# Stick-breaking heads: the triangle products from two float32r parts, in whole banks, at the end of their step

## What is computed

```python
z = jnp.einsum('bhtd,bhsd->bhts', qf, kf) * scale
mask = s_pos < t_pos
log_keep = jnp.where(mask, jax.nn.log_sigmoid(-z), 0.0)
later = lax.cumsum(log_keep, axis=3, reverse=True) - log_keep
w = jnp.where(mask, jnp.exp(jax.nn.log_sigmoid(z) + later), 0.0)
out = jnp.einsum('bhts,bhsd->bhtd', w, vf)
```

## Time and profile before

| | us |
|---|---|
| median of 3 runs | 3109.47 |
| lowest and highest | 3108.03, 3111.07 |
| the profiled execution | 3111.8 |
| its span, first to last instruction | 3110.0 |
| TensorE busy in the span | 3060.9 |
| VectorE, ScalarE, GpSimd busy | 1855.5, 1148.2, 1903.9 |
| mean granted TensorE clock | 0.997 |

### The profile page before, as it was taken

The page is one execution under the profiler, slowest core; times in us unless marked ns, Lnnn a source line. Parts: engine busy times, 40 slices in busy tenths (PEclk is TensorE's granted clock), DMA queues, the critical chain, the costliest instruction groups (busy, mean ns, idle before and its releaser), DMA issues.

```text
span 3110.0 us, 42623 instructions
## 1 busy us (share of the span) xinstructions
PE 3060.9 (98%) x15287; PEld 2585.1 (83%) x15287; DVE 1855.5 (60%) x3298; ACT 1148.2 (37%) x2064; POOL 1903.9 (61%) x1796
## 2 busy tenths in 40 slices
PE   8999999999999999999999999999999999999999
PEld 6877788887668888878777888999999997888887
DVE  7674544316765442250672236679857878987886
ACT  3455322102552221120554212434357763333333
POOL 7432666677337666766433566578875565667663
PEclk9999999999999999999999999999999999999999
DMA  7210222222212222222112222488888889999995
GB/s 229 73 41 28 102 95 95 95 95 102 75 42 102 95 95 95 95 102 95 68 55 75 69 95 106 166 284 300 299 303 310 331 317 371 374 375 362 360 361 205
DMA packets 153709, 539.26 MB, mean 173 GB/s; under 512 B 11155, under 2 KB 64564, under 8 KB 117172
## 3 DMA queue, kind: packets, MB, share of 16 engines
q1 hardware_dynamic: 97296, 334.78, 30.3%
q0 software_dynamic: 36864, 134.23, 11.8%
q10 hardware_dynamic: 19364, 67.72, 5.8%
HBM read 479.16 MB, written 57.40 MB: 173 GB/s over the span
## 4 chain that ended last, share of the span: by engine, by line
PE 93%; DVE 3%; DMA 1%; issue 1%; ACT 1%; SPq 1%; POOL 0%; ACTq 0%; DVEq 0%; POOLq 0%
PE banks L194 82%; PE banks L2831 3%; PE banks L2174 1%; PE banks L2212 1%; DMA weights_raw<-in_weights 1%; PE banks L1110 1%; PE banks L1197 1%; PE banks L1169 1%; PE banks L2191 1%; PE banks L1179 1%; PE banks L2775 1%; DVE memory L1887 0%; SPq L2712 0%; DVE memory L1882 0%; DVE memory L1873 0%
## 5 line engine op out<-in xcount | busy, mean ns | idle before, releaser
L194 PE MATMUL banks<-memory,weights_split 128*128 128x512 f32 (+1 forms) x9456 | 2070.7, 376 | 18.5 <-DVE memory L555 11.7
L194 PEld LDWEIGHTS banks<-memory,weights_split 128*128 128x128 f32 x9456 | 1714.8, 188 | 296.8 <-issue 37.5
L3405 POOL TENSOR_SCALAR weights_split<-weights_raw 128x512 fp32r<-128x512 f32 x576 | 374.8, 660 | 790.2 <-PE banks L194 397.1
L3410 POOL TENSOR_TENSOR weights_split<-weights_raw,weights_split 128x512 fp32r<-128x512 f32 x576 | 769.2, 1346 | 0.0
L3271 POOL TENSOR_TENSOR weights_split<-weights_raw,weights_split 128x512 fp32r<-128x512 f32 x384 | 506.2, 1341 | 302.9 <-ACT weights_split L3115 301.6
L194 PE MATMUL banks<-weights_split,memory 128*128 128x512 f32 (+1 forms) x2880 | 647.4, 386 | 0.6 <-POOL weights_split L3271 0.6
L194 PEld LDWEIGHTS banks<-weights_split,memory 128*128 128x128 f32 x2880 | 534.0, 188 | 110.3 <-POOL weights_split L3271 1.4
L3115 ACT ACTIVATE weights_split<-weights_raw 128x1024 fp32r<-128x1024 f32 x256 | 269.4, 1053 | 103.4 <-DMA weights_raw<-in_weights 66.9
L690 DVE TENSOR_TENSOR banks<-banks,memory 128x512 f32<-128x512 f32 x88 | 61.3, 699 | 231.9 <-PE banks L194 231.8
L2903 DVE CUSTOM_DVE_ANT_0 memory<-memory,banks 128x1024 f32<-128x1024 f32 x128 | 154.7, 1210 | 63.0 <-DMA memory<-in_peer_u,memory 63.0
L3265 POOL DMA_INDIRECT memory<-in_peer_v,memory x128 | 157.5, 1230 | 52.2 <-issue 25.4
(11 more groups left out here) (280 smaller groups left out, 2727.7 us busy)
## 6 DMA issues: line engine op xcount, KB each, us to landing
weights_raw<-in_weights SPq DMA_DIRECT2D x272, 1024.0 KB, 4.9
routing<-memory ACTq DMA_DIRECT2D x12, 2048.0 KB, 10.8
hidden<-memory ACTq DMA_DIRECT2D x62, 384.0 KB, 5.0
memory<-hidden SPq DMA_DIRECT2D x31, 768.0 KB, 12.8
memory<-routing SPq DMA_DIRECT2D x30, 768.0 KB, 10.5
window_rows<-memory ACTq DMA_DIRECT2D x1, 3064.0 KB, 26.5
chunk_rows<-memory ACTq DMA_DIRECT2D x1, 2556.0 KB, 12.1
residual<-in_x ACTq DMA_DIRECT2D x4, 512.0 KB, 8.6
```

The costliest lines, as they stand in the source:

```text
L194: last = k.nc.tensor.matmul(out, left[a], right[b], start=start and n == 0, stop=stop and n == 2, skip_group_check=True)
L3405: k.nc.gpsimd.tensor_scalar(cut(high, n * PIECE, PIECE), cut(raw, n * PIECE, PIECE), 1.0, 1.0, ALU.mult, ALU.mult).then_inc(k.high_made, 1)
L3410: k.nc.gpsimd.tensor_tensor(cut(low, n * PIECE, PIECE), cut(raw, n * PIECE, PIECE), cut(high, n * PIECE, PIECE).bitcast(F32), ALU.subtract ...
```

## The change

The softplus is split after it is made: ScalarE copies it to float32r (`softplus_high`, over the memory of the logarithms), and VectorE subtracts that from it in place (`softplus_low`). The constants of the triangle and of ones get float32r copies, made at t = 7. The triangle products take whole groups, that is banks, and two products per group, high and low, in place of one float32 product per band. They stand now in `stick_ones`' place, directly ahead of it at the end of the step. The first product of `stick_ones` for each band is also made of two float32r products; those with `behind_0` and `behind_1` stay. The weights of groups 1 and 2 wait for the third signal, since they are written over the high part.

```diff
--- before.py
+++ after.py
@@ -931,6 +931,12 @@
     q_part, k_part = common.work[0:2], common.work[2:4]
     with k.scope(at=B_AT):
         stick_high, head_low, head_high, stick_low = (units(4, F32R) for _ in range(4))
+    with k.scope(at=X_AT + 29 * KB + 512):
+        exact = {name: k.take(P, F32R) for name in ('neg_tri', 'neg_ones')}
+    exact_made = k.sem("exact_constants")
+    with k.scope(at=X_AT + 16 * KB):
+        softplus_high, softplus_low = (k.take(1280, F32R) for _ in range(2))
+    parts_high, parts_low = k.sem("softplus_high"), k.sem("softplus_low")
     masks, weights = common.embedding, part
     with k.scope(at=SMALL_AT + 64):
         columns = Columns(k, 40)
@@ -1153,6 +1159,7 @@
             queries = odd_queries if h % 2 else queries_a[pair]
             if h == 0:
                 pe.wait_ge(halves_cleared, 1 + SB_HEADS // 2)
+                pe.wait_ge(exact_made, len(exact))
             if pair == 0:
                 made[9].await_read(pe)
             else:
@@ -1174,16 +1181,18 @@
                     last.then_inc(scored, 1)
 
         def stick_triangles(h):
-            pe.wait_ge(summed, 3 * h + 3)
-            for j in BANDS:
-                mm(band_bank(j), k.const("neg_tri"), band(softplus, j), start=False, stop=j == 3,
-                   skip_group_check=True)
+            pe.wait_ge(parts_low, 3 * h + 3)
+            for g, (at, size) in enumerate(GROUPS):
+                for side in (softplus_high, softplus_low):
+                    mm(group_bank(g), exact["neg_tri"], cut(side, at, size), start=False, stop=False,
+                       skip_group_check=True)
 
         def stick_ones(h):
             pe.wait_ge(behind_made, 3 * h + 3)
             for j in (0, 1, 2):
-                last = mm(cut(band_bank(j), P, P), k.const("neg_ones"), cut(band(softplus, j + 1), 0, P), start=False,
-                          stop=j == 2, skip_group_check=True)
+                for side in (softplus_high, softplus_low):
+                    last = mm(cut(band_bank(j), P, P), exact["neg_ones"], cut(band(side, j + 1), 0, P), start=False,
+                              stop=False, skip_group_check=True)
                 if j < 2:
                     last = mm(cut(band_bank(j), 2 * P, (2 - j) * P), k.const("neg_ones"), behind_1 if j else behind_0,
                               start=False, stop=True, skip_group_check=True)
@@ -1225,8 +1234,8 @@
                 cross(*use)
             advance(share)
             h, v = stick_at(t)
-            if v is not None and v != 1:
-                {0: stick_scores, 2: stick_triangles, 3: stick_apply}[v](h)
+            if v in (0, 3):
+                {0: stick_scores, 3: stick_apply}[v](h)
             advance(counts[t] - 2 * share)
             for i, u in heads_at(t):
                 if u == 11:
@@ -1234,6 +1243,7 @@
                 if u == 13:
                     turn_out(i)
             if v == 2:
+                stick_triangles(h)
                 stick_ones(h)
         for _ in work:
             pass
@@ -1365,6 +1375,11 @@
                              ALU.add).then_inc(behind_made, 1)
             dve.wait_ge(behind_made, 3 * h + 1)
             v_.tensor_tensor(cut(behind_0, P, P), cut(band(softplus, 1), 2 * P, P), behind_1, ALU.add).then_inc(behind_made, 1)
+            dve.wait_ge(behind_made, 3 * h + 3)
+            for g, (at, size_) in enumerate(GROUPS):
+                dve.wait_ge(parts_high, 3 * h + g + 1)
+                v_.tensor_tensor(cut(softplus_low, at, size_), cut(softplus, at, size_),
+                                 cut(softplus_high, at, size_).bitcast(F32), ALU.subtract).then_inc(parts_low, 1)
 
         def stick_low_part(h):
             rows, n = rows_of(h), h // 2
@@ -1519,9 +1534,14 @@
                 act.wait_ge(exp_neg, 3 * h + g + 1)
                 a.activation(cut(part, at, size), cut(part, at, size), ACT.Ln, bias=1.0).then_inc(log1p, 1)
 
+        def stick_parts(h):
+            for g, (at, size) in enumerate(GROUPS):
+                act.wait_ge(summed, 3 * h + g + 1)
+                a.activation(cut(softplus_high, at, size), cut(softplus, at, size), ACT.Copy).then_inc(parts_high, 1)
+
         def stick_weights(h):
             for g, (at, size) in enumerate(GROUPS):
-                act.wait_ge(exponents, 3 * h + g + 1)
+                act.wait_ge(exponents, 3 * h + (3 if g else 1))
                 a.activation(cut(weights, at, size), group_bank(g), ACT.Exp).then_inc(weighted, 1)
 
         def stick_high_part(h):
@@ -1559,6 +1579,9 @@
                     end_exponents(i)
                 if u == 9:
                     copy_k(i)
+            if t == STICK_AT - 2:
+                for name, tile in exact.items():
+                    a.activation(tile, k.const(name), ACT.Copy).then_inc(exact_made, 1)
             if t == STICK_AT:
                 rows.await_written(act)
             if v == 0:
@@ -1577,6 +1600,8 @@
                     silu(i)
                 if u == 13:
                     head_high_part(i)
+            if v == 1:
+                stick_parts(h)
             if t == 4:
                 evacuate_values(0, values_b)
             if t == 8:
```

## The result

The changed kernel takes 3132.8 us (median of 6 runs, 3130.6 to 3134.6) beside 3108.9 (3107.8 to 3111.1) for the kernel before on the same chip: ratio 1.0075, 95% interval 1.0065 to 1.0086, slower by some 24 us. The prediction was 3115.5 with 3107 to 3122.5 as its range: right in sign, wrong in size. The profiled execution has a span of 3129.4 us against 3110.0, 19.4 more. Of these 17.1 are there when TensorE leaves the woven loop (334.5 us against 317.4 at the first product behind it); the last 2 come behind 2600 us, where TensorE waits for split weights of the expert layer 1.4 and 1.3 us in this execution and 0.6 in that of the kernel before. Whether they belong to the change is not shown: one execution of each kernel was profiled.

A forecast was written before the change was run, and what follows sets the result against it. TensorE, busy 98% of the span, was taken to bound the kernel. Work (-4.5 + 0.6 + 2.2 + 1.1 + 3.2 = +2.6 us) and clock (+3.4) gave +6.0: median 3109.5 to 3115.5 us, range 3107 to 3122.5.

The forecast's parts named there:

- TensorE's saving: Each head: triangles 2.08 to 1.2 us, ones step unchanged at 1.24, together 2.44; gain 0.88 us a head.
- VectorE's and ScalarE's cost without contention: Step 2 of a head: three subtractions take VectorE 1.63 us; ScalarE's three copies cost nothing, 0.4 us to spare.
- Odd heads: Triangles wait for low parts 1.7, 2.7, 3.8, 4.1 us in heads 3, 1, 5, 7; losses 0.6, 1.1, 2.2, 3.2.
- the old slow stretch: Head 1, kernel before: 3.4 us at 1.2 GHz behind TensorE's 2.33 us stall at its HGRN product.
- the 1.77 us of the earlier trace: Head 7: longest 512-column VectorE form with two SBUF inputs, 1.772 us; makes the three subtractions 3.8 us.
- the clock: Behind the new stalls of heads 5 and 7: one 1.2 GHz stretch each, +3.4 us together; bounds none or three (5.1).
- the old waits of even heads: TensorE's waits on the softplus sums in even heads, 0.95 us over the kernel, go away.
- Four even heads: Heads 0, 2, 4, 6: no wait on low parts; 3.5 us plus 0.95 of old waits, 4.5 us gained.
- my sum: Work +2.6 us and clock +3.4 us, in all +6.0 us.
- Clock stays up: Second rival: clock stays full in heads 5 and 7, 3112.1 us; chance 0.26.
- no stall: Third rival: TensorE never stands at the triangles, low parts ready before it arrives; -8.4 us, 3101; chance 0.07.
- The first rival: Narrow float32r products cost as much per column as float32: 0.62 us a head, 5.0 us more, 3120.5; chance 0.22.

The follow-up runs named there:

- experiment 2: Changed kernel without the three subtractions; the products on the low part read the high part again and wait for ScalarE's third copy: 3103.8 us, ratio 0.9977.
- experiment 3: Changed kernel with each subtraction replaced by an operation with one PSUM input that writes zeros as the low part: 3124.3 us, ratio 1.0047.
- Experiment 1: Kernel before with its float32 triangle products moved to the end of their step, ahead of the ones products, nothing split: 3107.1 us, ratio 0.9994.
- experiment 5: Changed kernel with the move undone: float32r triangle products at the old place, ahead of the last dense products and the attend: 3139.2 us, ratio 1.0097.
- Experiment 4: Changed kernel with 67 useless float32r products ahead of the triangles of heads 1, 3, 5, 6 and 7: 3122.3 us, ratio 1.0040.
- experiment 7: Changed kernel with triangles and ones moved behind the first dense product of the next step: 3120.5 us.
- 9: Changed kernel with all products not needing the low part issued ahead of the wait, low products last, waiting per group: 3115.0 us, ratio 1.0018.
- 10: Kernel of experiment 9 with the low products behind the first dense product of the next step: 3116.0 us, ratio 1.0020.
- 11: Kernel of experiment 10 with the low products behind the second dense product too in heads 1, 5, 6 and 7: 3113.0 us, ratio 1.0013.
- 12: Kernel of experiment 11 with VectorE's HGRN multiplications ahead of the next difference in step 2, query evacuation behind both: 3108.95 us, ratio 0.9996.
- 6: Kernel before with the copies and subtractions added; float32 triangles don't read them, only the head's weights on ScalarE wait for them: 3114.7 us, ratio 1.0021.
- 8: Changed kernel with high-part triangle products at the old place and low-part ones at the end of the step: 3119.3 us.

## Why the prediction was wrong

**TensorE's saving: right.** 2.44 us a head were forecast for the triangles and ones, 2.54 measured. The narrow float32r products cost 0.11 us as taken; the rival that made them as dear as float32 falls, by head 0 and by experiment 2.

**VectorE's and ScalarE's cost without contention: right.** The three subtractions take 1.63 us in head 0, and ScalarE's copies delay no triangle.

**Odd heads: right in kind, sizes near.** Waits of 1.94, 4.07 and 4.39 us in heads 3, 5 and 7 against 1.7, 3.8 and 4.1. Head 1 had 3.65 against 2.7: the old slow stretch, which I took as given ahead of the wait, did not come in this execution, so TensorE arrived earlier, and a new one came behind the wait. Head 7's size came from the 1.77 us of the earlier trace rows. The Trainium skill (SBUF — State Buffer, Who interferes with whom) says that a VectorE instruction with two SBUF inputs contends with a GpSimd instruction that reads SBUF; the trace agrees, 4.05 us in head 7 against 1.62 in experiment 3.

What each head cost, read from the start of the products that apply its weights, after less before, each head's by itself:

| head | forecast without the clock | measured | slow stretches in it, net of before |
|---|---|---|---|
| 0 | -0.9 | -0.9 | 0 |
| 1 | +1.1 | +2.7 | 0 (one ahead of the wait went, one behind it came) |
| 2 | -0.9 | +1.1 | 0 |
| 3 | +0.6 | +2.3 | 1 |
| 4 | -0.9 | -0.9 | 0 |
| 5 | +2.2 | +3.5 | 1 |
| 6 | -0.9 | +3.6 | 1 |
| 7 | +3.2 | +6.3 | 2 |

The forecast has another -0.95 for the old waits of even heads, 0.66 of it in head 6. A slow stretch is 1.7 us.

**The first step that failed is "Four even heads".** I worked out head 0 and carried its result to heads 2, 4 and 6. The gain of 0.88 held in head 0 and about in head 4, with waits of 0.19 and 0.44. In head 2 contention lengthened the subtractions to 2.46 us, TensorE waited 0.62 for them and the next HGRN product 0.96; in head 6 the wait was 3.62. The move brought that about: with the triangles behind the dense products GpSimd's burst, which splits the next slot of weights when TensorE has left it, starts earlier against VectorE's chain. I had counted the burst where it already lay beside the additions (heads 5 and 7), not where the change would bring it. Experiment 1 shows it for the move alone, in head 6 (0.2 us ahead of the end of the sums, not 2.9 behind) and in head 2 (0.9 behind, not 3.0); experiment 5, which puts the triangles back, has the burst 4 us or more behind the sums in both heads, subtractions of 1.63 us, and in head 6 a shorter wait in spite of an earlier place. Heads 2 and 6 together were forecast at -1.8 and came to +4.7, a slow stretch of 1.7 included: some 4.8 us of the miss without it.

**The second is the clock, and it weighs more.** I took one slow stretch behind each of two heads (+3.4, with three as the bound). There were six pieces, and the old one was not among them: +8.5, so 5.1 more than forecast; head 1's 1.6 us come on top, because the old piece lay where a wait would have hidden it and the new one does not. Experiment 4 shows the clock's part by itself, 8.6 us. My mistake was to reason from two stalls of before, 2.33 us followed by a slow stretch and 1.91 by none, as if the length decided between them. The experiments show that there it does not (below).

**The rivals.** "Clock stays up" is refuted by the profile after, "no stall" by its 18.9 us of waits. The first rival, dear narrow products, is the one whose time (3120.5) came nearest, and its mechanism is refuted above. My range ended at three slow stretches and did not hold the burst moving to another head; the loop alone came 11.1 us above my sum, and these two steps make up that difference but for half a microsecond.

What stays open: whether the last 2 us of the profiled difference, the waits for split weights, belong to the change; 4 to 5 us by which the medians' difference (23.9) exceeds that of the two profiled executions (19.4), where the clock has a part, since four of the six runs of the kernel after have a mean clock of 0.993 and the profiled one 0.994, and 0.001 of the span is 3.1 us; and the part of experiment 7's gain that its waits and clock don't explain.

## What to carry to other kernels

A product that is cheaper on the bounding engine is paid for by the engine that prepares its operand: set arrival against readiness head by head, and ask anew in each what a moved instruction does to the other engines' bursts, rather than carry one head's result to its like. Issue what does not need the late operand first and wait per piece; then look at what the preparation pushes back in its own queue, where the wait goes next. A stall on TensorE can have a second price in the clock behind it; here useless products in the gap removed 8.6 of 10.3 us of it, and work that has to be done anyway is better still (experiments 9 to 12).

## What the runs showed of the hardware

- **The lower clock comes in pieces of one size.** The full-clock time lost in the loop, in the 14 profiled executions, one of each kernel, was 0, 1.7, 3.4, 5.1, 8.5, 10.3 or 12.0 us: multiples of 1.7, that is 3.4 us at 1.2 GHz each.
- **Whether a stall of about 2 us is followed by one is not set by its length.** The stall at the HGRN product of head 1 is in all 14, 2.33 to 2.35 us long. In 7 of them a slow stretch follows (before, experiments 3, 4, 6, 7, 8 and 10), in 7 none (after, 1, 2, 5, 9, 11 and 12). Behind the stall of 1.89 to 1.93 us in head 5 it came in 3 (6, 9 and 11). Stalls of 2.43, 2.02, 2.68 and 3.07 us in experiment 5 were followed by none. Others as short had one or two, for instance 1.94 us (head 3 of the kernel after), 2.62 (the same head in experiment 5), 1.85 (experiment 9), 2.93 (experiment 7), and in experiments 11 and 12 two stalls of 0.91 and 1.23 us close together. Each of the 11 stalls of 3.39 us and over had one or two in it or behind it: 3.39, 3.62, 3.65, 3.73, 3.81, 4.05, 4.07, 4.33, 4.39, 4.76 and 5.74. What decides below that is not shown; nor is it shown whether another execution of the same kernel has its pieces at the same places.
- **Contention works on both engines.** Two SBUF inputs on VectorE: three operations in 2.46, 3.40 and 4.05 us beside GpSimd's split, 1.63 without it; one input from PSUM: 1.62 in the same burst. GpSimd's pair of L3435 (L3436 in experiment 3) took 3.35 us beside VectorE's subtractions in head 7, 2.51 beside the form with a PSUM input.
